# Multiscale pooling of a two-block transformer kernel: the window means as a product with a constant band on TensorE, after the group matrices

## The reference, cut to what matters

```python
for g, win in enumerate(POOL_WINDOWS):
    lo = jnp.clip(t - win // 2, 0, l)
    hi = jnp.clip(t + win - win // 2, 0, l)
    ...
    mean = (csg[:, hi] - csg[:, lo]) / (hi - lo).astype(jnp.float32)[None, :, None]
    outs.append(mean - uf[..., sl])
dlt = jnp.stack(outs, axis=2).astype(u.dtype)
y = jnp.einsum("blgc,gcd->blgd", dlt, w).reshape(b, l, d)
return y * scale
```

## Time and profile before

| | us |
|---|---|
| median of 3 runs (lowest, highest) | 2654.69 (2652.11, 2656.16) |
| the profiled execution, first to last instruction | 2656.3 |
| PE busy | 2499.0 (94%) |
| DVE busy | 1725.4 (65%) |
| ACT busy | 960.6 (36%) |

### The profile page before, as it was taken

How to read it: one execution, slowest core, us unless ns; L and a number is a source line. 1 busy time by engine, 2 the same in 40 slices (tenths; PEclk the granted TensorE clock), 3 DMA queues, 4 the chain that set the end, 5 groups by cost and what they waited for, 6 DMA issues and landing times.

```text
span 2656.3 us, 26794 instructions
## 1 busy us (share of the span) xinstructions
PE 2499.0 (94%) x10562; PEld 1899.7 (72%) x10562; DVE 1725.4 (65%) x2192; ACT 960.6 (36%) x1262; POOL 103.3 (4%) x186
## 2 busy tenths in 40 slices
PE   6998769999994999999999999999999999999997
PEld 3884338788882788887774578888877646788886
DVE  7886588865658854668985585554689855733334
ACT  4324335422422422333554343222346543422221
POOL 0111000000000000000000000000000000000000
PEclk8998779999996999999999899999999998999999
DMA  7461002455552354553220124454522210223222
GB/s 279 154 229 40 16 16 103 150 173 179 168 175 86 111 187 168 168 175 127 80 90 23 39 103 159 159 187 158 177 95 86 78 36 30 82 91 107 96 87 80
DMA packets 66807, 315.25 MB, mean 119 GB/s; under 512 B 7128, under 2 KB 12632, under 8 KB 45817
## 3 DMA queue, kind: packets, MB, share of 16 engines
q1 hardware_dynamic: 41624, 222.29, 24.1%
q0 software_dynamic: 25056, 91.24, 10.5%
HBM read 311.40 MB, written 2.10 MB: 118 GB/s over the span
## 4 chain that ended last, share of the span: by engine, by line
PE 82%; DVE 13%; issue 1%; DMA 1%; ACT 1%; SPq 0%; DVEq 0%; ACTq 0%
PE psum L533 23%; PE psum L535 23%; PE psum L534 23%; PE psum L829 2%; DVE squares L1344 1%; PE psum L848 1%; DVE rstd L1296 1%; DVE x_lo L1339 1%; PE psum L858 1%; PE psum L847 1%; DVE w_lo L1445 1%; DMA big<-in_ada_first 1%; PE psum L880 1%; PE psum L666 1%; PE psum L725 1%
## 5 line engine op out<-in xcount | busy, mean ns | idle before, releaser
L533 PE MATMUL psum<-x_hi,w_hi 128*128 128x512 f32 x1968 | 782.5, 398 | 15.8 <-DVE squares L1394 10.7
L535 PE MATMUL psum<-x_hi,w_lo 128*128 128x512 f32 x1968 | 767.5, 390 | 0.0
L534 PE MATMUL psum<-x_lo,w_hi 128*128 128x512 f32 x1968 | 767.5, 390 | 0.0
L1445 DVE TENSOR_TENSOR w_lo<-w_raw,w_hi 128x2048 fp32r<-128x2048 f32 (+1 forms) x192 | 418.8, 2181 | 340.7 <-ACT w_hi L980 338.4
L980 ACT ACTIVATE w_hi<-w_raw 128x2048 fp32r<-128x2048 f32 (+1 forms) x192 | 350.5, 1825 | 528.7 <-DMA w_raw<-in_w 528.6
L533 PEld LDWEIGHTS psum<-x_hi,w_hi 128*128 128x128 f32 x1968 | 370.3, 188 | 110.5 <-issue 22.3
L534 PEld LDWEIGHTS psum<-x_lo,w_hi 128*128 128x128 f32 x1968 | 370.5, 188 | 78.9 <-issue 5.3
L535 PEld LDWEIGHTS psum<-x_hi,w_lo 128*128 128x128 f32 x1968 | 370.1, 188 | 78.3
L533 PE MATMUL psum<-hidden_hi,w_hi 128*128 128x512 f32 x912 | 356.4, 391 | 0.0
L535 PE MATMUL psum<-hidden_hi,w_lo 128*128 128x512 f32 x912 | 354.9, 389 | 0.0
L534 PE MATMUL psum<-hidden_lo,w_hi 128*128 128x512 f32 x912 | 354.8, 389 | 0.0
(11 more groups left out here) (389 smaller groups left out, 2544.6 us busy)
## 6 DMA issues: line engine op xcount, KB each, us to landing
w_raw<-in_w SPq DMA_DIRECT2D x160, 1024.0 KB, 4.9
ada_w<-in_ada POOLq DMA_DIRECT2D x164, 512.0 KB, 4.0
w_raw<-in_w SPq DMA_DIRECT2D x32, 704.0 KB, 4.1
big<-in_ada_first SPq DMA_DIRECT2D x12, 768.0 KB, 14.1
big<-in_ada POOLq DMA_DIRECT2D x10, 512.0 KB, 5.2
extra<-in_w_uq SPq DMA_DIRECT2D x8, 384.0 KB, 3.3
residual<-in_xT SPq DMA_DIRECT2D x2, 1024.0 KB, 9.6
cond_row<-in_c_row SPq DMA_DIRECT2D x4, 512.0 KB, 5.3
```

What stands on the lines that cost most here:

```text
L533: mm(o, w_h, x_h, start=first, stop=False)
L534: mm(o, w_h, x_l, start=False, stop=False)
L535: return mm(o, w_l, x_h, start=False, stop=last)
L1445: v.tensor_tensor(wl[:, r, 0:n], raw[:, r, 0:n], wh[:, r, 0:n].bitcast(f32), ALU.subtract).then_inc(w_split.sem, 1)
```

## The change

- DVE keeps one instruction per tile, the scaling, now in place in `big[:, k, :]`; ACT adds the shift in place. The shifted sums, the product with the inverse counts, the subtraction, the padded rows and their two memsets are gone, and with them DVE's wait for the two transfers.
- PE applies the group matrix first (`pool_mix`), with the input as the stationary operand: for each of five spans of 128 times (start 0, 104, 216, 328, 384) two products of 128x256, so the result has times on partitions. Ten products a group, in banks 0, 1, 2 or 3, 4, 7.
- ACT copies them from PSUM to `pool_z` (`pool_turn`: two copies of 128x512 and one of 128x256 a group).
- PE then applies the band (`pool_window`): per output tile five products, four with 112 columns and one with 64, against a constant table of mean less identity, into bank 5 or 6 as before.
- The table, `pool_band`, 128x2240 fp32 (1.15 MB), takes the place of `pool_inv` (1 MB), and is loaded between the weights of the second and the third stage of `mlp1`, behind a wait for the rotary angles, since it lies over their position row. `pool_w` is still loaded when `mlp1` is done, but now ahead of `cond_row`.

The diff, cut where lines only set names or repeat:

```diff
+POOL_COLS = P - 2 * PAD
+POOL_N = -(-T // POOL_COLS)
+def pool_from(i):
+    return min(max(POOL_COLS * i - PAD, 0), T - P)
...
@@ sync @@
-            for st in mlp1:
-                load_stage(st, 4 if st is mlp1[0] else 0)
+            load_stage(mlp1[0], 4)
+            load_stage(mlp1[1])
+            eng.wait_ge(S("angles2").sem, 1)
+            load(small[:, 0:5, :]..., a["pool_band"], "pool_loaded")
+            load_stage(mlp1[2])
+            load_stage(mlp1[3])
...
             eng.wait_ge(slot_done.sem, stages[9].slot0)
+            load(big[:, 12:16, :], a["pool_w"]..., "pool_loaded")
             eng.wait_ge(ada_read.sem, LATE_N + MODS_N)
             load(cond_row[:], a["c2_row"], "row_loaded")
-            load(big[:, 8:12, :], a["pool_inv"]..., "pool_loaded")
-            load(big[:, 12:16, :], a["pool_w"]..., "pool_loaded")
@@ tensor @@
-            for n in range(KD):
-                g, m = n // 2, n % 2
-                eng.wait_ge(S("pooled").sem, 2 * g + 2)
-                eng.wait_ge(S("pool_used").sem, max(0, n - 1))
-                for k in range(2):
-                    at = (2 * g + k) * 256 + m * P
-                    ins = mm(B(5 + n % 2), big[:, 12 + at // T, at % T:at % T + P], big[:, 2 * g + k, :],
-                             start=k == 0, stop=k == 1)
+            def pool_mix(g):
+                eng.wait_ge(S("pool_shifted").sem, 2 * g + 2)
+                if g >= 2:
+                    eng.wait_ge(S("pool_turned").sem, 3 * (g - 1))
+                for i in range(POOL_N):
+                    for k in range(2):
+                        at = (2 * g + k) * 256
+                        ins = mm(ps[:, pool_banks[g % 2][i // 2], i % 2 * 256:i % 2 * 256 + 256],
+                                 big[:, 2 * g + k, pool_from(i):pool_from(i) + P], big[:, 12 + at // T, at % T:at % T + 256],
+                                 start=k == 0, stop=k == 1)
+                    if i % 2 == 1 or i == POOL_N - 1:
+                        ins.then_inc(S("pool_mixed").sem, 1)
+            def pool_window(n):
+                g = n // 2
+                eng.wait_ge(S("pool_turned").sem, 3 * (g + 1))
+                eng.wait_ge(S("pool_used").sem, max(0, n - 1))
+                for i in range(POOL_N):
+                    to = pool_cols(i)
+                    ins = mm(ps[:, 5 + n % 2, to], pool_z[:, i, n * P:(n + 1) * P], pool_band[:, g, i, 0:to.stop - to.start],
+                             start=True, stop=True)
                 me.count(ins.then_inc(S("pool_out").sem, 1), S("pool_out"))
+            pool_mix(0)
+            for g in range(len(POOL)):
+                if g + 1 < len(POOL):
+                    pool_mix(g + 1)
+                pool_window(2 * g)
+                pool_window(2 * g + 1)
@@ scalar @@
+            def pool_turn(g):
+                for j, bank in enumerate(pool_banks[g % 2]):
+                    eng.wait_ge(S("pool_mixed").sem, 3 * g + j + 1)
+                    n = min(2, POOL_N - 2 * j)
+                    act(pool_z[:, 2 * j:2 * j + n, g * 256:(g + 1) * 256], B(bank, n * 256)...,
+                        ACT.Copy).then_inc(S("pool_turned").sem, 1)
+            pool_turn(0)
+            for g in range(len(POOL)):
+                if g + 1 < len(POOL):
+                    pool_turn(g + 1)
+                for n in (2 * g, 2 * g + 1):
+                    eng.wait_ge(S("pool_used").sem, n + 1)
+                    tile_part(n, sites[1])
@@ vector @@
-            eng.wait_ge(L("pool_loaded").sem, L("pool_loaded").next(me, 2))
...
-                for w in POOL[:g + 1]:
...
             for k in range(KD):
+                me.count(v.scalar_tensor_tensor(big[:, k, :], h[:, k, :], gain[:, k:k + 1], rstd[:], ALU.mult, ALU.mult)
+                         .then_inc(S("pool_scaled").sem, 1), S("pool_scaled"))
```

More of the change, by code:

```diff
@@ L441, in _ @@
             eng.wait_ge(slot_done.sem, stages[9].slot0)
+            load(big[:, 12:16, :], a["pool_w"].rearrange("p (a n) -> p a n", a=4), "pool_loaded")
             eng.wait_ge(ada_read.sem, LATE_N + MODS_N)
             load(cond_row[:], a["c2_row"], "row_loaded")
-            load(big[:, 8:12, :], a["pool_inv"].rearrange("g p t -> p g t"), "pool_loaded")
-            load(big[:, 12:16, :], a["pool_w"].rearrange("p (a n) -> p a n", a=4), "pool_loaded")
             for st in mlp2:
@@ L1181, in _ @@
             for k in range(KD):
-                x = pads[:, 3 * (k % 2), PAD:PAD + T]
                 eng.wait_ge(S("pool_scaled").sem, k + 1)
[L1184 to L1187, removed]
+                act(big[:, k, :], big[:, k, :], ident_f, bias=mods[:, 1, k:k + 1]).then_inc(S("pool_shifted").sem, 1)
+            def pool_turn(g):
+                for j, bank in enumerate(pool_banks[g % 2]):
+                    eng.wait_ge(S("pool_mixed").sem, 3 * g + j + 1)
+                    n = min(2, POOL_N - 2 * j)
+                    act(pool_z[:, 2 * j:2 * j + n, g * 256:(g + 1) * 256], B(bank, n * 256).rearrange("p (i n) -> p i n", n=256),
+                        ACT.Copy).then_inc(S("pool_turned").sem, 1)
[6 more added lines that the diff above has]
+                    tile_part(n, sites[1])
             scaled_his(sites[1])
@@ L1881, in _ @@
             inverse_root()
-            eng.wait_ge(L("pool_loaded").sem, L("pool_loaded").next(me, 2))
[L1883 to L1889, removed]
-            for k in range(KD):
[L1891 to L1898, removed]
-                for w in POOL[:g + 1]:
[L1900 to L1904, removed]
-                        edge = (1, T + 2 * Z)
-                    else:
-                        lo, hi = edge[0] + d, edge[1] - d
-                        me.count(v.tensor_tensor(dst[:, lo:hi], cur[:, lo - d:hi - d], cur[:, lo + d:hi + d], ALU.add).then_inc(me.done.sem, 1), me.done)
-                        eng.wait_ge(*me.own())
-                        edge = (lo, hi)
-                    cur, nxt = dst, 3 - nxt
-                me.count(v.tensor_tensor(t1[:], cur[:, Z:Z + T], big[:, 8 + g, :], ALU.mult).then_inc(me.done.sem, 1), me.done)
-                eng.wait_ge(*me.own())
-                me.count(v.tensor_tensor(big[:, k, :], t1[:], row[:, Z:Z + T], ALU.subtract).then_inc(S("pooled").sem, 1), S("pooled"))
-                eng.wait_ge(*me.own())
+            for k in range(KD):
+                me.count(v.scalar_tensor_tensor(big[:, k, :], h[:, k, :], gain[:, k:k + 1], rstd[:], ALU.mult, ALU.mult).then_inc(S("pool_scaled").sem, 1), S("pool_scaled"))
+            eng.wait_ge(*me.own())
             root_free()
@@ L2177, in layouts @@
     f["decay"] = np.exp(-lin[:, None] * np.abs(deltas)[None, :]).astype(np.float32)[halves]
-    inv_n = np.stack([1.0 / (np.clip(t + n - n // 2, 0, T) - np.clip(t - n // 2, 0, T)) for n in POOL]).astype(np.float32)
-    f["pool_inv"] = np.ascontiguousarray(np.broadcast_to(inv_n[:, None, :], (4, P, T)))
+    band = np.zeros((P, len(POOL), POOL_N, POOL_COLS))
+    for g, w in enumerate(POOL):
+        lo, hi = np.clip(t - w // 2, 0, T), np.clip(t + w - w // 2, 0, T)
+        full = ((t[:, None] >= lo) & (t[:, None] < hi)) / (hi - lo) - np.eye(T)
+        for n in range(POOL_N):
+            to = pool_cols(n)
+            band[:, g, n, 0:to.stop - to.start] = full[pool_from(n):pool_from(n) + P, to]
+    f["pool_band"] = np.ascontiguousarray(band.reshape(P, -1).astype(np.float32))
     f["pool_w"] = np.ascontiguousarray(i["pool_w"][0].reshape(4, 2, P, 256).transpose(2, 0, 1, 3).reshape(P, 2048))
```

11 lines of the change are left out of this document (7 added, 4 removed).

## The result

| | before | changed |
|---|---|---|
| median of 9 runs (lowest to highest), us | 2660.25 (2648.30 to 2663.31) | 2643.06 (2632.33 to 2651.07) |
| span of the profiled execution, us | 2656.3 | 2641.2 |
| from the reciprocal's start behind the first MLP to the row sums of the next norm, us | 57.88 | 41.29 |

The ratio of the times, the median over the nine pairs of runs, is 0.9945, with a 95% interval of 0.9930 to 0.9961: 14.6 us saved, 10.4 to 18.6. (The two medians of the table lie 17.2 us apart; the ratio of pairs is used here.) The predicted saving was 15.7, a ratio of 0.9941. The nine runs of before lie 5.6 us above the three from which the prediction started, and so the changed kernel's median lies 4.1 above the predicted 2639.0, inside the range of 2635.5 to 2646.

The account below looks back on a forecast made before the run. Bound: the pooling, where PE stands idle while DVE makes window sums. The next norm's row sums come 15.7 us earlier (853.2 against 868.92), so 2654.7 - 15.7 = 2639.0 us, range 2635.5 to 2646.

Parts of the forecast that it names:

- first scaling, no transfer ahead of it: Pooling's start on DVE: no wait of 1.53 us for transfers, first scaling at about 814.42 instead of 815.93.
- first mix product: PE's first group-matrix product in the pooling: two tiles shifted at 816.72, so it starts at 816.77.
- end of mix(0) and mix(1): PE's group-matrix products of groups 0 and 1, ten each: the first group ends at 824.05, the second at 828.35.
- read of tile 4: DVE's read of output tile 4 in the pooling, 0.30 us after PE goes on to the next tile: 843.25.
- from there to the row sums: DVE's unchanged order behind tile 4's read, 2.30 us a tile: row sums 9.94 us later, at 853.2.
- The clock term: PE's first products in the pooling: 5.95 us at the lower clock level, 1.2 GHz, until 822.72.
- The window products: PE's band products in the pooling: 0.24 us each, 1.2 us per output tile, 9.6 us for 40.
- The scalings: DVE's one instruction per tile at the pooling's start: 0.77 us each, the last six tiles never late.
- the copies of group 2: ACT's PSUM copies of group 2 in the pooling: end some 0.5 us behind that group's mix products, not binding.
- the band's load: 1.15 MB in SP's queue during the first MLP: costs nothing; without cover at most 5 us, once.
- rival 4: After the pooling: a later transfer or the modulation rows absorb the gain; 2652 us, chance 0.03.
- The other three: Pooling rivals: loads in series, 2652.7 us, 0.03; clock stays low, 2665, 0.04; dear window products or later rise, 2644, 0.16.

Follow-up runs that it names:

- double: Changed kernel with each window product made twice (80 instead of 40); reciprocal to row sums 47.27 us against 41.29.
- loads_first: Kernel before with only the table of inverse counts and the matrices loaded ahead of cond_row; reciprocal to row sums 56.05 us against 57.88.
- interleaved: Kernel before with VectorE's sums kept, but its reads of the output tiles put between them; reciprocal to row sums 54.93 us against 57.88.
- late: Changed kernel with the band's table loaded behind pool_w when the first MLP is done; reciprocal to row sums 41.28 us against 41.29.

## Why the prediction was right

Its steps, in microseconds after the reciprocal's start:

| step | predicted | measured |
|---|---|---|
| first scaling, no transfer ahead of it | 3.38 | 3.39 |
| first mix product | 5.73 | 5.70 |
| clock at the lower level after that | 5.95 | 5.03 |
| end of mix(0) and mix(1) | 17.31 | 16.91 |
| ten window products | 2.40 | 2.18 |
| ten mix products at the upper level | 4.30 | 4.37 |
| read of tile 4 | 32.21 | 31.35 |
| from there to the row sums | 9.94 | 9.94 |
| row sums | 42.16 | 41.29 |

- **What sets the pace.** The prediction split the pooling where the bound changes: PE up to the read of tile 4, DVE from there. Both halves held, and the second to a hundredth, because it is the same instructions in the same order as before. PE's waits of 1.00 us at window 7 and 0.82 at the row sums are where it put them.
- **The clock term was too large.** I took the longer of the two delays that the trace of before showed. The measured 5.03 leaves 0.46 us. It is not a constant: 5.03 here and 3.6 in double, where the mix products are the same, 3.9 in loads_first's second burst and 2.8 in interleaved's last. What decides it no run shows, so that the term came out within half a microsecond is luck; a range of 3 to 6 us would have been right.
- **The window products were priced at 0.24 and cost 0.218.** The nearest row said 0.27 for 128 columns and the loads' floor 0.22. The floor was the price; 25 products make 0.5 us. The mix product's 0.437 instead of 0.43 takes 0.2 back.
- **The scalings** follow at 0.67 us, not 0.77. It changes nothing: the mix needs two shifted tiles to begin, and the other six are never late.
- **Nothing else came up.** The transfer wait is gone, the copies of group 2 end 0.58 us behind mix(2) (some 0.5 predicted), the band's load stops nobody, and late shows that it could even stand behind the MLP.
- **The gain is kept.** The 96.5 us behind the second reciprocal are the same in all ten kernels, and the 504 us to the second attention the same before and after, which ends rival 4. The other three are ended by double and by the windows of the clock.
- **The absolute time is in the range partly by luck.** The range of 10.5 us allowed 2 us for the spread of the runs, taken from three runs. Nine runs of before spread over 15.0 us and nine of the changed kernel over 18.7, and four of those nine lie outside the range. The mechanism and its saving are what was forecast well, not the 2639.0.

The sum came out 0.9 us short by the trace (15.7 against 16.59) and 1.1 over by the ratio's middle (14.6), well inside its interval. The spans of the two profiled executions differ by 15.1, 16.6 less the 3.07 us lost ahead of the pooling, and 1.6 from later stages that didn't change.

## What to carry to other kernels

Find the point at which the bound passes from one engine to the other, and forecast each side from its own rows: the side whose instructions stay the same can be copied to the hundredth, and all the uncertainty is in the other. Shortening one side pays only until the other ends last (here 0.98 of 1.5 us). Where one engine stands idle because another works, moving that work over pays even if the first engine needs more instructions for it than it had: here PE got 8.8 us more in the stretch, DVE lost 25.8, and the stretch became 16.6 shorter. And a difference of a few microseconds is to be read in a stretch that begins and ends with fixed instructions, since the totals of this kernel can't tell it.

## What the runs showed of the hardware

**The spread between runs sits outside the MLPs.** From the reciprocal ahead of the first MLP to the one behind it the ten profiles have 351.02 to 351.08 us, but for double with 352.67, where the MLP's code is that of the others. The program's start up to the first of these takes 454.7 to 463.1, and the second attention 190.1 to 199.7, with the same code in all. Two windows of one execution, the kernel late, its second and its third attention:

```profile
1358.70:1548.80 190.10, 180.68 (x703) 113.06 (x702) 125.45 (x213) 74.51 (x164) 1.05 (x2) 0.99 0.17 56
2064.60:2264.20 199.60, 190.23 (x703) 117.54 (x702) 116.28 (x205) 74.53 (x164) 0.00 (x0) 0.94 0.14 45
```

The second and the third attention, 703 matmul instructions each, take 190.1 us where the mean granted clock was 0.99 and 199.6 where it was 0.94. An estimate from these two lines: 2% of 190.1 us at the lower level against 12% of 199.6 costs 10.1 us, and 9.5 were measured. In the changed kernel's profile the second attention took 193.5 us, in that of loads_first 199.7. That the clock is the cause there is argued from these windows, and what decides it wasn't tested. In the program's start it is less plain: from 22.3 us to the next norm's reciprocal again took 257.7 us at a mean clock of 0.94, and the changed kernel 262.0, from 22.5 us, at 0.95. Some of that difference has another cause, which wasn't found.

**A product with few columns costs its loads.** Trains of plain fp32 products, four of 112 columns and one of 64 by turns, take 0.218 us a product: two loads of 0.11 with everything else hidden. With 256 columns the same two loads are hidden and the product takes 0.437.

**Useless work can hold the clock.** Seven products of 512 columns, 6.2 us of TensorE in a wait of 6.6, gave back 2.50 us. In the bursts behind a pause that were followed, the rise came 2.8 (interleaved) to 5.95 us (before) after the burst's start, and interleaved's bursts of 3.75 us at 834.23 and 847.76 ran at the lower level from end to end. So here most of the work of a burst of 3 or 4 us is to be priced at the lower level.
